# Convolution, SSD tiles, group norm and mask product of a hybrid encoder layer placed as single steps between attention stages and linear pieces

## What is computed

```
h += 0.5 * SwiGLU_1(rmsnorm(h))
u  = rmsnorm(h); P = u @ w_in
     columns of P: SSD z | SSD x,B,C | SSD dt | q | k | v | forget | gates
o_ssm  = Mamba-2 SSD(z, silu(conv(xBC)), dt)      32 heads, 8 groups, state 128
o_attn = forgetting attention(q, k, v, log f)     16 heads
h += (sig(gate_ssm) * (o_ssm @ w_br_ssm) + sig(gate_attn) * (o_attn @ w_br_attn)) @ w_out
h += 0.5 * SwiGLU_2(rmsnorm(h)); final rmsnorm
```

## Time and profile before

| | |
|---|---|
| median of 3 runs | 2318.5 us (2315.66 to 2320.86) |
| profiled execution, first to last instruction | 2317.8 us; no further time is given for it |
| PE busy | 2110.8 us, 91% |
| DVE, ACT, POOL busy | 929.4, 767.7, 383.3 us |
| mean granted TensorE clock | 0.954 of full speed |
| HBM traffic | 81 GB/s over the span |

### The profile page before, as it was taken

One profiled execution on the slowest core, in us unless ns is written; L12 is line 12 of the kernel. 1 busy time (PEld: TensorE's weight loads), 2 busy tenths in 40 slices (PEclk: granted clock), 3 DMA queues, 4 the chain that ended last, 5 costly groups with the idle time before them and its releaser, 6 DMA issues. The chain is left out here.

```text
span 2317.8 us, 39197 instructions
## 1 busy us (share of the span) xinstructions
PE 2110.8 (91%) x14969; PEld 2029.3 (88%) x14969; DVE 929.4 (40%) x1516; ACT 767.7 (33%) x1317; POOL 383.3 (17%) x475
## 2 busy tenths in 40 slices
PE   4999999977989799979998897899999899999997
PEld 3999999967889788878987886699999799999996
DVE  2323232343772457245724672322344333232333
ACT  3321221233444344444444443332211232122122
POOL 1000000005543154315431541000000000000000
PEclk9999999988999899989998998899999999999999
DMA  3222322222215022502251223133323122222221
GB/s 99 73 91 73 90 73 79 66 82 83 80 51 164 29 73 70 164 29 73 70 163 30 71 71 122 50 94 100 123 90 125 45 73 91 73 82 81 73 73 41
DMA packets 223559, 190.31 MB, mean 82 GB/s; under 512 B 9776, under 2 KB 211584, under 8 KB 222144
## 3 DMA queue, kind: packets, MB, share of 16 engines
q1 hardware_dynamic: 219520, 173.53, 24.7%
q0 software_dynamic: 3360, 14.81, 2.0%
q10 hardware_dynamic: 544, 0.17, 0.0%
HBM read 169.16 MB, written 19.33 MB: 81 GB/s over the span
## 5 line engine op out<-in xcount | busy, mean ns | idle before, releaser
L1445 PE MATMUL ps<-xah,wh 128*128 128x296 f32 x2704 | 612.7, 308 | 37.2 <-DVE xal L1122 36.1
L1445 PE MATMUL ps<-xah,wl 128*128 128x296 f32 x2704 | 600.3, 304 | 0.0
L1445 PE MATMUL ps<-xal,wh 128*128 128x296 f32 x2704 | 596.8, 303 | 0.0
L1445 PEld LDWEIGHTS ps<-xah,wh 128*128 128x128 f32 x2704 | 446.8, 193 | 44.7 <-issue 31.6
L1445 PEld LDWEIGHTS ps<-xal,wh 128*128 128x128 f32 x2704 | 450.4, 193 | 0.0
L1445 PEld LDWEIGHTS ps<-xah,wl 128*128 128x128 f32 x2704 | 445.4, 192 | 0.4
L785 ACT ACTIVATE wh<-raw 128x2048 fp32r<-128x2048 f32 x92 | 175.6, 1908 | 304.2 <-PE ps L1445 300.1
L698 POOL TENSOR_TENSOR wl<-raw,wh 128x512 fp32r<-128x512 f32 (+1 forms) x160 | 199.8, 1261 | 406.2 <-ACT wh L793 405.6
L1116 DVE TENSOR_TENSOR wl<-raw,wh 128x2048 fp32r<-128x2048 f32 x93 | 213.2, 2292 | 120.0 <-ACT wh L785 97.5
L1445 PE MATMUL ps<-xbh,wh 128*128 128x296 f32 x960 | 211.2, 302 | 5.7 <-DVE xbl L1122 5.7
L1445 PE MATMUL ps<-xbh,wl 128*128 128x296 f32 x960 | 210.0, 300 | 0.0
(11 more groups left out here) (232 smaller groups left out, 2489.8 us busy)
## 6 DMA issues: line engine op xcount, KB each, us to landing
raw<-in_ffn_w_in_dram SPq DMA_DIRECT2D x88, 512.0 KB, 4.9
raw<-in_w_in_dram SPq DMA_DIRECT2D x80, 512.0 KB, 4.6
raw<-in_ffn_w_out_dram SPq DMA_DIRECT2D x32, 512.0 KB, 4.2
brow<-acs_rows SPq DMA_DIRECT2D x8, 1184.0 KB, 6.2
raw<-in_w_br_ssm_dram SPq DMA_DIRECT2D x16, 512.0 KB, 4.2
raw<-in_ffn_w_out_dram SPq DMA_DIRECT2D x16, 384.0 KB, 3.3
bias<-bias_rows SPq DMA_DIRECT2D x32, 160.0 KB, 3.9
os_spill<-yT SPq DMA_DIRECT2D x8, 592.0 KB, 3.3
```

Of the source, the lines that this page charges most:

```text
L1445: ins = pe.matmul(bank(b + a, HALF), w[:, slot, k, j * P:(j + 1) * P], x[:, k, a * HALF:(a + 1) * HALF], start=(k == 0 and w is wh and x i ...
```

## The change

convA becomes four steps and convB two: `tap0` (ACT), `tap` 1, 2 and 3 (DVE), `tanh` (ACT) and `conv` (DVE). s1 is cut before the mask product (`s1b` holds cbm and mb), and s3 is cut in three (`s3a` sums, reciprocals and roots; `s3b` the scaling of yg on DVE; `s3` the turn on PE and the copy on ACT). Each of them has a position of its own. In the attention window and in the first stretch, one convolution tile spans two pieces: tap 0 to 2 in one, tap 3, tanh and conv in the next. In an SSD window prep and the rest of the convolution go into pieces 0 and 1, the first s1 goes from piece 1 to piece 2, the last three tiles' steps share piece 5, s3's turn goes from the end of piece 6 into piece 7, s4 from position 11 to 18 of piece 7, and fetch from ahead of piece 8 to position 14 in it, behind the weight load that piece 8 triggers on SP. No instruction is added and none is left out.

```diff
+def conv_steps(g, j, ahead, at):
+    kinds = [("tap0",), ("tap", 1), ("tap", 2), ("tap", 3), ("tanh",), ("conv",)]
+    return tuple((pos, (kind[0], g, j, ahead) + kind[1:]) for pos, kind in zip(at, kinds))
+SPREAD = (8, 13, 19, None, None, None)
+NEXT = (None, None, None, 1, 3, 7)
 def first_pieces(ahead, within=lambda n, t: ()):
+    conv = {(1, 1): some(conv_steps(0, 0, ahead, SPREAD)),
...
-        if (n, t) == (2, 0):
-            order += [("convA", 0, 0, ahead), ("convA", 0, 1, ahead)]
...
 def ssd_window(duos, g):
-        0: [("prep", g), ("convA", g, 3, 0), ("convB", g, 2, 0), ("cst", g), ("convB", g, 3, 0)],
...
-        6: ((7, ("s3", g)), ),
-        7: ((3, ("s4", g)), ),
+        6: ((7, ("s3a", g)),),
+        7: ((1, ("s3b", g)), (9, ("s3", g)), (18, ("s4", g))),
...
+    if g == 0:
+        within[6] += conv_steps(1, 0, 0, (9, 11, 13, 16, 18, 20))
+        within[7] += conv_steps(1, 1, 0, (6, 10, 12, 14, 16, 20))
...
-                        for tap in range(1, 4):
-                            ins = dve.scalar_tensor_tensor(out=c, in0=xp[:, j, tap:tap + CO],
...
+                        i, j, tap = now + step[3], step[2], step[4]
+                        if tap == 1:
+                            dve.wait_ge(tap0_ready, i * 8 + (4 * g + j + 1))
+                        else:
+                            dve.wait_ge(dch, chain())
...
-                    elif kind == "s3":
+                    elif kind == "s3a":
                         act.wait_ge(rv_ready, i * 2 + (g + 1))
...
```

More of the change, by code:

```diff
@@ L146, in with_splits, with some @@
     return out
+def conv_steps(g, j, ahead, at):
[3 more added lines that the diff above has]
+NEXT = (None, None, None, 1, 3, 7)
+def some(steps):
+    return tuple(step for step in steps if step[0] is not None)
 def first_pieces(ahead, within=lambda n, t: ()):
+    conv = {(1, 1): some(conv_steps(0, 0, ahead, SPREAD)),
+            (2, 0): some(conv_steps(0, 0, ahead, NEXT) + conv_steps(0, 1, ahead, SPREAD)),
+            (2, 1): some(conv_steps(0, 1, ahead, NEXT) + conv_steps(0, 2, ahead, SPREAD))}
     order = []
@@ L153, in first_pieces @@
         n, t = piece[1:3]
-        if (n, t) == (2, 0):
-            order += [("convA", 0, 0, ahead), ("convA", 0, 1, ahead)]
-        if (n, t) == (2, 1):
-            order += [("convB", 0, 0, ahead), ("convA", 0, 2, ahead), ("convB", 0, 1, ahead)]
-        order.append(piece[:4] + (within(n, t),))
+        inner = tuple(sorted(within(n, t) + conv.get((n, t), ()), key=lambda x: x[0]))
+        order.append(piece[:4] + (inner,))
     return with_splits(order)
 def ssd_window(duos, g):
-    before = {
-        0: [("prep", g), ("convA", g, 3, 0), ("convB", g, 2, 0), ("cst", g), ("convB", g, 3, 0)],
-        6: [("rows", 1, 0)] * (g == 0),
-        7: [("convA", 1, 0, 0), ("convA", 1, 1, 0)] * (g == 0),
-        8: [("convB", 1, 0, 0), ("convA", 1, 2, 0), ("convB", 1, 1, 0)] * (g == 0) + [("fetch",)] * (g == 1),
-    }
@@ L171, in ssd_window @@
[L171 to L176, removed]
-        6: ((7, ("s3", g)), ),
-        7: ((3, ("s4", g)), ),
-    }
+    before = {6: [("rows", 1, 0)] * (g == 0)}
+    within = {
+        0: some(conv_steps(g, 2, 0, (None, None, None, 1, 3, 6)) + conv_steps(g, 3, 0, (7, 10, 14, 18, 22, None))) + ((20, ("prep", g)),),
+        1: some(conv_steps(g, 3, 0, (None,) * 5 + (6,))) + ((12, ("cst", g)), ),
+        2: ((6, ("s1", g, 0)), (16, ("s1b", g, 0))),
+        3: ((0, ("s1", g, 1)), (3, ("s2", g, 0)), (16, ("s1b", g, 1))),
+        4: ((0, ("s1", g, 2)), (3, ("s2", g, 1)), (16, ("s1b", g, 2))),
+        5: ((0, ("s1", g, 3)), (1, ("s2", g, 2)), (7, ("s1b", g, 3)), (9, ("s1", g, 4)), (10, ("s2", g, 3)), (16, ("s1b", g, 4)),
+            (20, ("s2", g, 4))),
+        6: ((7, ("s3a", g)),),
+        7: ((1, ("s3b", g)), (9, ("s3", g)), (18, ("s4", g))),
+        8: ((14, ("fetch",)),) * (g == 1),
+    }
@@ L180, in ssd_window @@
+    if g == 0:
+        within[6] += conv_steps(1, 0, 0, (9, 11, 13, 16, 18, 20))
+        within[7] += conv_steps(1, 1, 0, (6, 10, 12, 14, 16, 20))
+        within[8] += some(conv_steps(1, 2, 0, (6, 10, 16, None, None, None)))
     order = []
     for at, piece in enumerate(pieces(duos)):
-        order += before.get(at, []) + [piece[:4] + (tuple((3 * k + 2, inner) for k, inner in within.get(at, ())),)]
+        inner = tuple(sorted(within.get(at, ()), key=lambda x: x[0]))
+        order += before.get(at, []) + [piece[:4] + (inner,)]
```

30 lines of the change are left out of this document (18 added, 12 removed).

## The result

The changed kernel takes 2258.65 us (median of 4 runs, 2254.4 to 2259.47), the kernel before 2319.35 us beside it: a ratio of 0.9738, interval 0.9724 to 0.9752. The change gains 61 us. The forecast was 2247 us with 2212 to 2276 around it, so the side and the size hold, and 12 us of the expected gain are missing. The profiled execution has a span of 2257.8 us at a mean clock of 0.964.

A forecast was written before the change was run, and what follows sets the result against it. PE, busy 91%, was bound by waits on late DVE and POOL work and the half clock after them. Removing 110.4 us and adding 39 gains 71.4; from 2317.8, plus 0.7 for the median, 2247 us, range 2212 to 2276.

The forecast's parts named there:

- Attention: Loop's three attention windows: six long otok waits go, 40.3 us, with 19.7 us of half clock; overrunning taps add 2.
- the slot: DVE's idle time before an attention division, 1.05 to 2.50 us in undisturbed stages; a chained tap of 0.99 us fits.
- SSD windows: Waits for cv, sini, weight split and yg go, 34.5 us, plus 15.9 us of clock: 50.4 us removed before added costs.
- the weight split: PE's 3.7 us of waits for POOL's weight split in the SSD windows should go; no new wait there was priced.
- 15.9 us of half clock: SSD windows: PE runs 31.80 us at half clock after waits; 15.9 us counted as lost and expected back.
- The norm of a first group: A convolution tile before yg's scaling makes PE wait 3.6 us, plus 2.3 of clock, four times: 24 us added.
- PE comes later because the tiles hold it: Part of the rival without a wait at the first group's norm: that cost vanishes, 2223 us; chance 0.14.
- its own signs: Profile after: otok under 5 us, attention clock 1.00, cv, sini, split at most 2 each, yg waits only in first groups.
- Tiles: SSD tiles: mask product behind the previous tile's s2 costs first groups 2 us per window, 8 us; second groups nothing.
- Fetch: Last pass: the cache is sent some 5 us later, behind the weight load; PE waits 0 to 4 us, 2 taken.
- The table load: Before the norm's roots on ACT: it starts when the split before it is over, and the root follows.
- A slower kernel: Outcome in which the change makes the whole kernel slower; chance 0.04.

The follow-up runs named there:

- attention part alone: The change with the SSD windows put back into the order of the kernel before; 2260.45 us, ratio 0.9762 to the kernel before.
- two taps in a slot: The change with fetch back ahead of piece 8, and tap 1 moved next to tap 2 in attention windows and first stretch; 2249.04 us, ratio 0.9712.
- roots behind the splits: The change with the norm's sums, reciprocals, roots and the following tap moved behind piece 6's last weight-split quarter; 2258.17 us, ratio 0.9754.
- the scaling first: The change with fetch ahead of piece 8, roots behind the splits, and first groups' yg scaled before the next convolution tile; 2237.47 us, ratio 0.9661.
- the early mask product: The change with fetch ahead of piece 8, and each SSD tile's cbm and mb back beside the rest of s1; 2244.73 us, ratio 0.9688.

## Why the prediction was right, and where it was off

**Attention: right.** Forecast 60.0 us removed and 2 added; with the attention part alone the windows fell by 58.4. The forecast's 19.7 us are half of the 39.44 us at 0.50 of the earlier trace rows; no run shows this term by itself. What the runs show in its place: with the attention part alone PE's entry for `otok` fell by 39.3 us (41.6 to 2.3), the clock of the three windows went from 0.89 to 0.91 up to 0.99 to 1.00, and PE was busy in them for 259.14 us against 279.23, 20.1 us less, with 2040 matmuls against 2042. That half of the time at 0.50 is lost (here 19.7 us, in the SSD windows 15.9) is the author's estimate. In the kernel before, two linear matmuls take 0.49 us from start to start at 0.50 (786.97 to 787.46) and 0.27 us at 1.00 (874.48 to 874.75), by which 45% of it is lost, 17.7 of the 39.44 us. The six waits and the half clock behind them were the bound, as read in the earlier trace rows. The reading of the slot was off: 1.05 us is not the least of the undisturbed stages. In the same windows of the kernel before others show 0.27 to 0.93 us, for instance

```profile
741.55 0.16 DVE L1253 RECIPROCAL rinv<-rsum 80x1 f32<-80x1 f32 x1 [0.27 <-PE ps L1565]
```

A tap of 0.99 us would not fit there. The change has its taps in later stages, where behind each of them DVE still idles 0.31 us or more before the division; and, as two taps in a slot show, the division may even start without any idleness. That the taps fell on stages with room is not what the prediction had read.

**SSD windows: right in direction, too large.** The forecast's net was 110.4 - 60.0 - 24 - 8 - 3 - 2 = 13.4 us gained, and 3 came. By PE's entries: yg gave 12.4, cv 8.4 and sini 7.1, 27.9 us, and 7.9 us less at half clock behind the waits another 4.0, counted at half as in the forecast. `wl` took 14.4, the cache 4.7, cbm and mb 3.6 (4.1 against 0.5); 22.7 us. The difference is 9 us. What takes it down to 3 is not shown: in the two profiles the returns of the loop cost 2 us more ("issue", 7.6 against 5.6), and the last attention had some 37 us at half clock against some 26, a figure that moves from run to run (below).

**The step that failed** is the weight split: the sum has no term for the new waits at it. The forecast says "so the waits for cv, sini and the weight split (8.4 + 7.1 + 3.7) should go", and these did go. The four old waits for the split stood ahead of the first piece of a second group, here in the kernel before:

```profile
887.28 0.38 PE L1457 MATMUL ps<-wh,xah 128*128 128x256 f32 x1 [1.05 <-POOL wl L698]
```

But eight new ones, 18.1 us, stand ahead of piece 7 of every SSD window. The same paragraph had a reason in hand: one root "is taken earlier, ahead of three of four weight splits" was booked as a gain for yg and never as a loss for the split, with its 1.28 us of table load. The run with the roots behind the splits gives its size: `wl` fell to 6.7 us, so 11.4 us come from roots and tap standing ahead of quarters, all 7.1 us of the first groups and 1.1 of the 2.8 us in each second group. The other 1.7 us in each second group had been covered by the old norm wait: before, PE stood 3.0 us for yg at the end of piece 6 while POOL finished the quarters.

```profile
926.70 5.03 POOL L698 TENSOR_TENSOR wl<-raw,wh 128x512 fp32r<-128x512 f32 x4 [4.36 <-ACT wh L793]
```

```profile
932.72 1.24 PE L1509 MATMUL ps<-ident,yg 128*128 128x128 f32 x10 [3.00 <-DVE yg L1367]
```

Take the norm wait away, and the wait behind it shows. Of the 15.9 us of half clock that were to come back, 4.0 did, as most of it now stands behind the new waits.

**The norm of a first group: right in mechanism, covered in fact.** Forecast 3.6 us of wait and 2.3 of clock in each of four; the change shows 1.5 us twice. The chain was right (7.4 us against 7.2), and the rival "PE comes later because the tiles hold it" was half right: PE came later, held not by the tiles but by `wl`. With roots behind the splits the forecast wait is there, 2.8 to 3.1 us four times, and with the scaling first it is gone. By its own signs the prediction is half borne out here: it asked for four waits of 2 to 5 us, there are two of 1.5, and in two passes of four the norm is reached without one.

**Luck.** That 2247 came within 12 us of the measured time is in part luck. The 18.1 us of new waits for `wl` stood at nothing, the norm of the first groups at 24 us for 2.9, and the two errors offset each other.

**Small terms.** Tiles, 8 us forecast: cbm and mb came to 4.1 us, half of them in second groups, where nothing was expected, and the early mask product gained 6 (by the ratios, whose intervals are 4 to 5 us wide on each side). Fetch, 2 us forecast out of 0 to 4: 4.7 us of wait, and 5 us by the ratios. The 5 us of later issue were right; the slower landing (8.3 us for 3.6) was not in the sum. The table load: the forecast counted its 1.28 us and nothing more; the change shows the load of 1.28 us at 841.02, 0.01 us after the split, the roots at 842.31 and 842.43 and tap 0 at 842.52, so that was right.

**A slower kernel**, to which the prediction gave 0.04, did not come: in first groups' windows the clock was 0.92 to 1.00.

## What to carry to other kernels

When a wait is taken away, ask what that wait was covering: look behind it, on every engine, for the next thing that the released engine will need, and when that thing is ready now. A step that is moved on one engine's list moves ahead of something, and that something needs a price too; a gain on one line of the sum can be a loss on another. And before steps are spread one by one, try how many of them fit into one gap: here two did.

## What the runs showed of the hardware

The last attention, alone on PE and with 20 short waits for `pt`, ACT's copy of the turned probabilities (12.5 us in all, the longest 0.8), ran in the same kernel with 64.85 us in one piece at half clock in one execution (window 154.1 us) and with no piece over 13.7 us in another (138.2 us). PE was busy for 56.80 of these 64.85 us, and the granted clock was 0.50 throughout. A single profile of a kernel with such a tail says little about the last per cent of its time; in second groups and attention the windows ahead of the tail agree to 0.4 us between the two.

Of the 96 taps of the change 29 took over 0.9 us, up to 1.79, and each of the 29 lay beside at least 0.44 us of POOL's tensor-by-tensor work; the other 67 took less and lay beside 0.61 us of it or less. So the same instruction on DVE took up to 1.79 us beside POOL's work, against a median of 0.84 over all 96. That POOL is the cause was not tried by an edit.
